# Fetching the rows of the second expert table whole, 8 KB a partition, in place of in halves of 4 KB

## What is computed

```
pre = jnp.einsum('tkd,td->tk', expert_u[i_blk], x_blk).astype(jnp.float32)
act = jax.nn.gelu(pre, approximate=False) * g_blk
return jnp.einsum('tk,tkd->td', act.astype(x_blk.dtype), expert_v[i_blk])
```

## Time and profile before

| | |
|---|---|
| median of three runs | 2115.3 us (2114.73 to 2115.97) |
| the profiled execution | 2115.16 us, of which its span is 2113.3 us |
| TensorE busy | 2046.6 us, 97% of the span |
| VectorE busy | 1636.4 us, 77% |
| ScalarE busy | 1084.7 us, 51% |
| GpSimd busy | 725.6 us, 34% |
| mean granted TensorE clock | 0.986 |
| moved by DMA | 496.19 MB, 235 GB/s over the span |

### The profile page before, as it was taken

One profiled execution on the slowest core, in us unless ns is written; L12 is line 12 of the kernel. 1 busy time (PEld: TensorE's weight loads), 2 busy tenths in 40 slices (PEclk: granted clock), 3 DMA queues, 4 the chain that ended last, 5 costly groups with the idle time before them and its releaser, 6 DMA issues.

```text
span 2113.3 us, 38239 instructions
## 1 busy us (share of the span) xinstructions
PE 2046.6 (97%) x12266; PEld 1875.8 (89%) x12266; DVE 1636.4 (77%) x2501; ACT 1084.7 (51%) x1450; POOL 725.6 (34%) x423
## 2 busy tenths in 40 slices
PE   7999999879999999999999999999999999999997
PEld 7888778878789999999999999999999899999885
DVE  6885776885557888888888656888889788888755
ACT  6543566234434755545554544555555555555454
POOL 0030200000000878788888860233232233343000
PEclk9999998899999999999999999999999999999999
DMA  5655558206544777777777776899999889999453
GB/s 195 252 182 185 170 169 304 95 16 227 196 170 170 212 207 209 208 208 209 209 209 207 216 244 243 308 352 343 344 347 347 291 304 332 356 339 330 167 180 139
DMA packets 171795, 496.19 MB, mean 235 GB/s; under 512 B 48560, under 2 KB 48976, under 8 KB 169808
## 3 DMA queue, kind: packets, MB, share of 16 engines
q1 hardware_dynamic: 117056, 413.39, 56.6%
q0 software_dynamic: 51200, 67.25, 12.0%
q10 hardware_dynamic: 3472, 14.78, 1.9%
HBM read 476.31 MB, written 19.04 MB: 234 GB/s over the span
## 4 chain that ended last, share of the span: by engine, by line
PE 83%; DMA 6%; DVE 6%; ACT 1%; issue 1%; DVEq 1%; SPq 0%; ACTq 0%
PE ps L260 27%; PE ps L265 15%; PE ps L1883 14%; PE ps L1888 7%; PE ps L286 5%; PE ps L280 5%; PE ps L281 5%; DMA raw<-in_v_table 4%; DVE lo L240 2%; DMA arena<-in_u_table,few_pick 1%; PE ps L1778 1%; PE ps L362 1%; ACT hi L234 1%; PE ps L1786 1%; PE ps L1734 1%
## 5 line engine op out<-in xcount | busy, mean ns | idle before, releaser
L234 ACT ACTIVATE hi<-raw 128x1024 fp32r<-128x1024 f32 x724 | 767.6, 1061 | 866.7 <-PE ps L260 390.6
L240 DVE TENSOR_TENSOR lo<-raw,hi 128x1024 fp32r<-128x1024 f32 x724 | 891.6, 1235 | 349.2 <-ACT hi L234 323.9
L260 PE MATMUL ps<-act_pair,hi 128*128 128x448 f32 (+1 forms) x2816 | 654.5, 374 | 0.0
L1621 POOL DMA_INDIRECT gate_map<-gate_in_sb x256 | 471.2, 1840 | 407.7 <-DVEq L1386 332.1
L260 PEld LDWEIGHTS ps<-act_pair,hi 128*128 128x128 f32 x2816 | 504.5, 189 | 49.3
L265 PEld LDWEIGHTS ps<-act_pair,lo 128*128 128x128 f32 x2816 | 371.9, 191 | 19.0 <-DVE lo L240 3.9
L265 PE MATMUL ps<-act_pair,lo 128*128 128x224 f32 (+1 forms) x2816 | 375.3, 276 | 2.0 <-DVE lo L240 2.0
L1883 PE MATMUL ps<-stage,hi 128*128 128x448 f32 x1024 | 232.7, 368 | 4.0 <-ACT hi L234 2.6
L1883 PE MATMUL ps<-act_pair,hi 128*128 128x448 f32 x1024 | 229.7, 366 | 1.4 <-ACT hi L234 1.4
L1638 POOL DMA_INDIRECT arena<-in_u_table,few_pick x64 | 104.2, 1627 | 310.2 <-DVE keep L1436 273.4
L1883 PEld LDWEIGHTS ps<-stage,hi 128*128 128x128 f32 x1024 | 183.6, 189 | 18.9 <-issue 3.3
(11 more groups left out here) (253 smaller groups left out, 1681.4 us busy)
## 6 DMA issues: line engine op xcount, KB each, us to landing
raw<-in_expert_u SPq DMA_DIRECT2D x256, 512.0 KB, 3.5
raw<-in_v_table SPq DMA_DIRECT2D x256, 512.0 KB, 6.7
raw<-in_w_in_cols SPq DMA_DIRECT2D x64, 512.0 KB, 3.3
raw<-in_w_in_rows SPq DMA_DIRECT2D x48, 512.0 KB, 3.3
raw<-in_w_out SPq DMA_DIRECT2D x32, 512.0 KB, 3.8
raw<-in_w_pq SPq DMA_DIRECT2D x32, 512.0 KB, 3.4
raw<-in_w_gate SPq DMA_DIRECT2D x32, 512.0 KB, 3.4
gate_map<-stage SPq DMA_DIRECT2D x1, 14336.0 KB, 41.5
```

The costliest lines, as they stand in the source:

```text
L234: act.activation(hi[:, use, :], raw[:, slot, :], ACT.Copy).then_inc(hi_ready, 1)
L240: dve.tensor_tensor(lo[:, use, :], raw[:, slot, :], hi[:, use, :].bitcast(F32), ALU.subtract).then_inc(lo_ready, 1)
L260: mm = pe.matmul(first_tokens(out_ap), hi[:, use, d8 * P:(d8 + 1) * P], first_tokens(act_pair[:, d, :]), start=(d == 0), stop=False)
L1621: pool.indirect_dma_start(gate_map, bass.IndirectOffsetOnAxis(ap=place[0:n, unit, r:r + 1], axis=0), gates_out[0:n, unit, r:r + 1], None, ...
```

## The change

The first table's fetches stay as they are. For the second table a step becomes one indirect DMA of 128 whole rows of 8 KB (1 MB) into one of two whole buffers, which take the same room as the four half buffers. VectorE's two operations of a step stay where they are in the list; both wait for the same DMA. GpSimd issues the fetch of step r when VectorE is done with both halves of step r - 2. The index of a whole row is half of that of its left half row, so it is worked out once: three small operations on VectorE over 128 x 32 numbers, with two drains, at the start of half 0, ahead of `apply_gates(0)`.

```
-        few_slots = [few_rows[:, 0:TILE], few_rows[:, TILE:D], region(4608, TILE), region(4608 + TILE, TILE)]
+        few_slots = [few_rows[:, 0:TILE], few_rows[:, TILE:D]]
+        few_whole = [few_rows, region(4608, D)]
...
-                rows_in = few_slots[slot]
-                dve.wait_ge(few_landed[slot], 16 * landed)
+                if n < FEW_STEPS:
+                    rows_in = few_slots[slot]
+                    dve.wait_ge(few_landed[slot], 16 * landed)
+                else:
+                    rows_in = few_whole[slot][:, c]
+                    dve.wait_ge(few_whole_landed[slot], 16 * landed)
...
+            dve.tensor_copy(few_act[:], few_index[:, 0])
+            dve.drain()
+            dve.tensor_scalar(few_act[:], few_act[:], 0.5, None, ALU.mult)
+            dve.drain()
+            dve.tensor_copy(few_ids[:], few_act[:]).then_inc(few_ids_ready, 1)
             apply_gates(0)
...
-            for n in range(2 * FEW_STEPS):
-                r, table = n % FEW_STEPS, u_table if n < FEW_STEPS else v_table
+            for n in range(FEW_STEPS):
                 for q in range(2):
-                    slot, _ = few_slot(n, q)
-                    m = 2 * (n - FEW_STEPS) + q
-                    if m >= FEW_SLOTS:
-                        pool.wait_ge(few_done, 2 * n + q - FEW_SLOTS + 1)
-                    elif m >= 2:
-                        pool.wait_ge(stage_lo_ready, CHUNKS + 14)
-                    elif n >= 1:
+                    if n >= 1:
                         pool.wait_ge(few_done, 2 * n + q - 1)
...
+            pool.wait_ge(few_ids_ready, 1)
+            for r in range(FEW_STEPS):
+                if r == 1:
+                    pool.wait_ge(stage_lo_ready, CHUNKS + 14)
+                else:
+                    pool.wait_ge(few_done, 2 * (FEW_STEPS + max(r - 1, 0)))
+                pool.indirect_dma_start(few_whole[r % 2], None, v_table,
+                                        bass.IndirectOffsetOnAxis(ap=few_ids[:, r:r + 1], axis=0)
+                                        ).then_inc(few_whole_landed[r % 2], 16)
```

More of the change, by code:

```diff
@@ L79 @@
 AHEAD = 2
-FEW_SLOTS = 4
 AB_ROUND = IN_CHUNKS // 2 - 2
@@ L154, in build @@
         few_act = sb("few_act", [P, FEW_STEPS])
+        few_ids = sb("few_ids", [P, FEW_STEPS], I32)
         keep = sb("keep", [P, C_KEEP])
@@ L214, in few_slot @@
                 return q, n + 1
-            m = 2 * (n - FEW_STEPS) + q
-            return m % FEW_SLOTS, m // FEW_SLOTS + 1 + (FEW_STEPS if m % FEW_SLOTS < 2 else 0)
+            m = n - FEW_STEPS
+            return m % 2, m // 2 + 1
         def hold(eng, name, s, value):
@@ L493, in build @@
                                                         sem("few_read"))
-        few_rows_in, x_few_ready, few_landed = sem("few_rows_in"), sem("x_few_ready"), [sem(f"few_landed{b}") for b in range(FEW_SLOTS)]
+        few_rows_in, x_few_ready, few_landed = sem("few_rows_in"), sem("x_few_ready"), [sem(f"few_landed{b}") for b in range(2)]
         scales_written = sem("scales_written")
+        few_ids_ready, few_whole_landed = sem("few_ids_ready"), [sem(f"few_whole_landed{b}") for b in range(2)]
         few_done, few_pre, few_gelu = sem("few_done"), sem("few_pre"), sem("few_gelu")
@@ L1626, in _ @@
             pool.wait_ge(x_few_ready, 2)
-            for n in range(2 * FEW_STEPS):
-                r, table = n % FEW_STEPS, u_table if n < FEW_STEPS else v_table
+            for n in range(FEW_STEPS):
                 for q in range(2):
-                    slot, _ = few_slot(n, q)
-                    m = 2 * (n - FEW_STEPS) + q
-                    if m >= FEW_SLOTS:
-                        pool.wait_ge(few_done, 2 * n + q - FEW_SLOTS + 1)
-                    elif m >= 2:
-                        pool.wait_ge(stage_lo_ready, CHUNKS + 14)
-                    elif n >= 1:
-                        pool.wait_ge(few_done, 2 * n + q - 1)
-                    pool.indirect_dma_start(few_slots[slot], None, table.rearrange("e (h f) -> (e h) f", h=2),
-                                            bass.IndirectOffsetOnAxis(ap=few_index[:, q, r:r + 1], axis=0)
-                                            ).then_inc(few_landed[slot], 16)
+                    if n >= 1:
+                        pool.wait_ge(few_done, 2 * n + q - 1)
+                    pool.indirect_dma_start(few_slots[q], None, u_table.rearrange("e (h f) -> (e h) f", h=2),
+                                            bass.IndirectOffsetOnAxis(ap=few_index[:, q, n:n + 1], axis=0)
+                                            ).then_inc(few_landed[q], 16)
+            pool.wait_ge(few_ids_ready, 1)
[7 more added lines that the diff above has]
+                                        ).then_inc(few_whole_landed[r % 2], 16)
             pool.wait_ge(final_landed, 16)
```

## The result

The changed kernel takes 2121.09 us in the median of 18 runs (2116.2 to 2129.19), the kernel before 2115.74 in the same number (2112.85 to 2119.56): a ratio of 1.0027 with a 95% interval of 1.002 to 1.0034. It is slower by some 5.4 us, a little over the 0.2% that can be told from no change. The profiled execution took 2122.52 us; its span is 2120.7 us, 7.4 more than before. Of the 7.4 us between the two profiled executions, 6.3 lie in half 1: from its first matmul to its last it takes 334.7 us in place of 328.4 (1649.6 to 1978.0 us in the kernel before). Half 0 starts 1.2 us later and is 0.4 shorter, and what follows half 1 is 0.3 longer.

A forecast was written before the change was run, and what follows sets the result against it. TensorE was taken to bound the kernel, with DMA having under a tenth to spare. Index +0.7, fetch waits +0.3 and 2 MB load +1.0 made +2.0 us on 2115.16, so 2117.2 us; range 2113.4 to 2125.

The forecast's parts named there:

- the likeliest case: Whole kernel: no measurable change, 2117.2 us, own range 2114 to 2119.5, chance 0.60.
- the second rival: Half 1: bursts of 8 KB rows delay tiles, leaving ScalarE waiting; +4 to +9 us, about 2121, chance 0.16.
- What bounds the kernel: Second table's stretch: TensorE bounds it, losing only 2.31 us; DMA engines have under a tenth to spare.
- the hole: Half 1 at 1809 to 1832 us, during the 2 MB load: a tile lands late and TensorE loses 2.3 us.
- The clock is granted in full: Second table's stretch, 1655 to 1968 us: TensorE's pace is also the fastest.
- What it takes away: Second table's fetches: some 54 us of GpSimd issuing and half the packets; worth nothing, engine work taken as unchanged.
- The index: Start of half 0, VectorE ahead of `apply_gates(0)`: three operations and two drains, 0 to +1.0 us, taken +0.7.
- The fetch's landing: Half 1: a 1 MB fetch lands in 10.2 us, against 11.0 us from issue to first use.
- A few waits: VectorE in half 1: a few waits for fetches, each under 2 us; +0.3 us in all, 0 to +3.
- The failed step: Tile stream in half 1: late tiles need median landing from 6.6 to near 8 us; outside the sum.
- the 2 us cushion: Half 1: `hi` and `lo` are made some 2 us ahead of use, absorbing a late VectorE or tile.
- The 2 MB load: Half 1: longer fetch rows beside this load delay a tile; +1.0 us, bounds -2.3 to +2.5.

The follow-up runs named there:

- the index alone: Kernel before plus only the three small index operations and two drains ahead of `apply_gates(0)`, result unused; ratio 1.0007 (0.9998 to 1.0016).
- its moving early: Changed kernel with only the index operations moved to the end of the first table's stage; ratio 1.0022 (1.001 to 1.0034) to the kernel before.
- without the load: 2 MB load of `h_spill` left out, output differs: changed kernel 2126.19 us, ratio 1.0012; kernel before 2119.02 us, ratio 0.9972.
- the pieces: 2 MB load cut into eight 256 KB pieces, one per round of four tiles: changed kernel 1.0011, kernel before 0.9994, both to the kernel before.
- with the index early: Changed kernel with the 2 MB load in eight pieces and index operations moved to the first table's stage end; 2120.23 us, ratio 1.0003 to before.
- The pairs of 4 KB fetches: Changed kernel with each step fetched as two back-to-back DMAs of 128 half rows; ratio 1.0039 (1.0024 to 1.0055) to the kernel before.
- the pairs with pieces: Changed kernel with two half-row DMAs per step and the 2 MB load in eight pieces; ratio 1.0011 (0.9993 to 1.0028) to the kernel before.
- the kernel with the load a round later: Changed kernel with the 2 MB load and the load of p issued four tiles (10 us) later; ratio 1.0038 (1.0026 to 1.005) to before.
- the changed kernel on the last chip: Changed kernel unaltered, rerun as reference on another chip: 2131.75 us against 2124.93 for the kernel before, ratio 1.0034 (1.0021 to 1.0047).

## Why the prediction was right or wrong

The range held (2113.4 to 2125.0), and the likeliest case, 2117.2, was 3.9 us too low and the time outside that case's own range (2114 to 2119.5): it came out by the second rival, "the tiles come late", which had said about 2121, +4 to +9, with a chance of 0.16.

*What bounds the kernel.* Right: TensorE at full pace with a thin DMA spare, and nothing to gain beyond the 2.31 us of the hole. No variant of the change beat the kernel before. "The clock is granted in full" holds inside the windows of the earlier trace rows; they begin at 1655 us, and the clock falls at 1650 (last section).

*What it takes away.* Right to count nothing: the engine time per byte of the fetches fell by 1%, and GpSimd's 49 us less busy (109.72 to 61.06 us from 1655 to 1968) moved nothing. The packets fell by 4603, not by some 4096: beside its 128 rows a fetch has 16 small packets of its own, and 32 fetches fewer save 512 of these (67 fetches of 144 packets are the 9648 of the earlier trace rows).

*The index.* +0.7 predicted; 0.75 us of TensorE's time in the profile. Shown by the index alone and by its moving early; the time of the index alone, +1.5 us by the ratio (-0.4 to +3.4), agrees and is no sharper.

*The fetch's landing.* 10.2 us predicted, 9.8 to 10.2 in the medians of the six profiles with whole rows that have it. A few waits, each under 2 us: 3, of 2.8 us in all, in the profile after; up to 8.5 us in all and 3.1 us each in the others. Right in the main, and by the rows that it was worked out from: between the engine work alone (9.5) and a second 512 KB (10.8). The estimate that the prediction made from the figures of the Trainium skill (DMA: Bandwidth & Descriptors, Anatomy of one DMA), 9.5, is a little low; these runs decide for 10.0.

*The failed step* is the one on tiles. The sum had no term for the tile stream outside the 2 MB load; it was left to the argument of the rival that "the 2 us cushion" had never been used up but at one place. The cushion is used up by the slow tiles, and the step priced a shift of the median landing, from 6.6 to near 8, which did not come (6.5 to 6.9 in the profiles with whole rows). The same bytes asked for in lumps of 1 MB leave the median and lengthen the slow end: ScalarE's waits for tiles in half 1 are 35 to 52 us in the kernels with the fetches of before and 70 to 104 us in every kernel with whole rows. The prediction had the burst itself right, 2.5 us in an engine where it was 1.3; it gave its cost to the median of all tiles and not to the one tile in about four that is issued just behind a fetch. That term should have been about +5, not 0.

*The 2 MB load.* +1.0 predicted, with a bound of +2.5; TensorE lost 5.26 us in place of 2.31 there and some 1.7 more by the clock, so +4.6 in the profile. In that execution the term was mis-sized, and the clock was missing from it. As a cost of whole rows it is not shown at all: on the one chip where all four kernels ran, whole rows cost as much without the load (7.2 us) as with it (6.8). The prediction's 11 us for the load stand in no row (it lands after 13.3), and its turn between single rows is not how the engines served the fetches. Against this, the pieces brought the changed kernel to 1.0011 on one chip, where the changed kernel itself did not run, and with the index early to 1.0003 on another; there the runs scatter by more than these differences, and the chips differ (the kernel before has medians of 2116.39, 2118.10 and 2124.93 us on them). How much the pieces win with whole rows is open. What all profiles with whole rows agree on is the late tiles.

*The mechanism behind the late tiles.* Shown: whole rows make them, with the load or without it; the rows of a fetch of 1 MB take the engines nearly whole for some 2 us, and the tiles issued just behind it are the late ones. That the half step less of lead does it is unlikely, as VectorE waits for whole rows for 8.5 us at most. Not separated: the length of a row and the size of a fetch, since no run had 8 KB rows in fetches of 512 KB. The pairs of 4 KB fetches lose 8 us in time, and their tiles keep only 15% of the engines in the 2 us of a pair, in the median; but in that profile ScalarE waits no more than before, and in the one of the pairs with pieces the fetches themselves are late. So the pairs show that 4 KB rows issued in this order are no cure, and not that their loss is the same one. The rule of the Trainium skill (DMA: Bandwidth & Descriptors, Queues, rings and completion order), that an engine changes queue only at packet boundaries, would give such bursts if the eight rows of a fetch make one packet; the traces agree with the burst, 86.5% of the engines against the two thirds that turns of single rows would give, but do not show what ends a turn.

## What to carry to other kernels

Where the DMA engines are over nine tenths busy beside a compute bound stream, as here, look at the largest lump of the other transfers: it is what a tile issued behind it has to wait for. Put the slow end of the landings, not their median, against the time the stream allows; here fetches of 512 KB, 4.2 us apart, stayed within it and fetches of 1 MB did not. A large one-off load costs in either kernel, at one place; the profiles with the load in pieces have no such stop, though the times did not show the gain clearly. Count matmuls in a fixed stretch and not only TensorE's idle time, since short stops and a lowered clock hide in what counts as busy.

## What was not expected of the hardware

After a single stop of 4.06 us TensorE's granted clock fell from full speed (2.4 GHz) to means of 0.83 and 0.75 over the next two stretches of 4 us, so in part to its lower level (1.2 GHz), and eight matmuls took 2.73 us in place of 1.79; in the kernel before, stops of 1.36 and 0.94 us at that place left it at 1.00, and so did four small ones in the kernel with the load a round later. But the length of one stop does not decide it: the changed kernel on the last chip, with none over 1.93 us, went to 0.83 and 0.75 as well, and the pairs of halves with pieces, with stops up to 2.93 us, stayed at 1.00.

The clock also falls where the halves meet, in either kernel, and not in every execution. In the kernel before it is 0.78 and 0.79 in two stretches of 4 us from 1650 us, and 0.74 and 0.83 from 1978, where half 1 ends; at 1649.60 TensorE had stood 0.81 us, and its first eight matmuls of half 1 take 4.37 us; the changed kernel on the last chip has 0.57 and 0.58 from 1658; the kernel before without the load, whose TensorE stands 1.10 us there with 4.09 for the first eight, and the changed kernel with the pieces have neither. By the clock column such a fall is 1.7 to 3.4 us, an estimate, so two of them are over half of the loss that this document is about, and likely a part of the scatter between executions.

Two indirect fetches of 512 KB back to back kept VectorE waiting 22.7 us in one profile and 2.2 in another, single fetches of 1 MB under the same waits never more than 8.5 us.
